# Shifting the operands of the dense layers against the weights in SBUF, and halving the products of one projection

## The reference

```
for i in range(2):                       # first block
    h = h + mixer_i(h)                   # RWKV + Hyena, then neighbourhood attention
    u = dwconv(rmsnorm(h) @ w_up)        # 1024 -> 5632, "conv_ffn"
    h = h + (gelu(u[:, :2816]) * u[:, 2816:]) @ w_down      # 2816 -> 1024
    h = h + sigmoid(rmsnorm(h) @ w_gate) * (p[i] @ w_proj)  # "ple": 1024 -> 1024, 256 -> 1024
for l in range(2):                       # second block
    x = x + gt1 * (attention(...) @ w_out)
    h = rms_norm(x) * (1 + sc2) + sh2
    x = x + gt2 * (square(relu(h @ w_mlp_in)) @ w_mlp_out)  # 1024 -> 4096 -> 1024, "mlp"
```

## Time and profile before

| | |
|---|---|
| time, median of 2 runs | 3125.95 us (3125.25 to 3126.65) |
| span of the profiled execution | 3120.8 us, on the one core |
| what the median has beyond that span | 5.15 us |
| PE busy | 2937.9 us, 94% |
| PE weight loads busy | 2328.9 us, 75% |
| DVE busy | 1717.0 us, 55% |
| ACT busy | 1294.5 us, 41% |
| HBM read | 280.57 MB, 91 GB/s over the span |

### The profile page before, as it was taken

How to read it: one execution, slowest core, us unless ns; L and a number is a source line. 1 busy time by engine, 2 the same in 40 slices (tenths; PEclk the granted TensorE clock), 3 DMA queues, 4 the chain that set the end, 5 groups by cost and what they waited for, 6 DMA issues and landing times. The chain is left out here.

```text
span 3120.8 us, 50278 instructions
## 1 busy us (share of the span) xinstructions
PE 2937.9 (94%) x21510; PEld 2328.9 (75%) x21510; DVE 1717.0 (55%) x2343; ACT 1294.5 (41%) x1998; POOL 120.0 (4%) x215
## 2 busy tenths in 40 slices
PE   7997777899999999999999899999999999999999
PEld 5764666678887777778888786678888876678887
DVE  5436665467674485657674468553333477442333
ACT  3232443243334433643233446645243446553241
POOL 0200000010000000000000010100000101000000
PEclk9998888899999999999999999999999999999999
DMA  4220000255652222245652230022233320123322
GB/s 148 81 75 13 4 4 4 82 161 191 193 153 94 88 81 95 82 132 179 219 172 91 70 108 31 1 81 95 95 95 108 90 71 1 35 89 107 95 95 81
DMA packets 223981, 287.99 MB, mean 92 GB/s; under 512 B 7967, under 2 KB 163911, under 8 KB 217616
## 3 DMA queue, kind: packets, MB, share of 16 engines
q1 hardware_dynamic: 213728, 226.26, 23.2%
q0 software_dynamic: 8448, 54.34, 5.2%
q10 hardware_dynamic: 1584, 4.19, 0.4%
HBM read 280.57 MB, written 2.10 MB: 91 GB/s over the span
## 5 line engine op out<-in xcount | busy, mean ns | idle before, releaser
L232 DVE TENSOR_TENSOR weights_low_all<-weights,weights_high_all 128x2048 fp32r<-128x2048 f32 x195 | 446.6, 2291 | 476.6 <-ACT weights_high_all L226 468.9
L226 ACT CAST weights_high_all<-weights 128x2048 fp32r<-128x2048 f32 x195 | 372.1, 1908 | 542.8 <-PE ps L240 542.8
L238 PE MATMUL ps<-ffn_h_high,weights_high_all 128*128 128x512 f32 x704 | 275.4, 391 | 0.9 <-DVE weights_low_all L232 0.9
L240 PE MATMUL ps<-ffn_h_high,weights_low_all 128*128 128x512 f32 x704 | 274.0, 389 | 0.0
L239 PE MATMUL ps<-ffn_h_low,weights_high_all 128*128 128x512 f32 x704 | 274.0, 389 | 0.0
L238 PE MATMUL ps<-mlp_h_high,weights_high_all 128*128 128x512 f32 x512 | 200.9, 392 | 0.4 <-DVE weights_low_all L232 0.3
L239 PE MATMUL ps<-mlp_h_low,weights_high_all 128*128 128x512 f32 x512 | 199.7, 390 | 0.0
L240 PE MATMUL ps<-mlp_h_high,weights_low_all 128*128 128x512 f32 x512 | 199.6, 390 | 0.0
L238 PE MATMUL ps<-weights_high_all,mlp_hid_high 128*128 128x512 f32 x512 | 199.2, 389 | 0.0
L239 PE MATMUL ps<-weights_low_all,mlp_hid_high 128*128 128x512 f32 x512 | 199.2, 389 | 0.0
L240 PE MATMUL ps<-weights_high_all,mlp_hid_low 128*128 128x512 f32 x512 | 199.2, 389 | 0.0
(11 more groups left out here) (562 smaller groups left out, 6189.4 us busy)
## 6 DMA issues: line engine op xcount, KB each, us to landing
mod_w<-in_w_mod POOLq DMA_DIRECT2D x48, 1024.0 KB, 5.3
weights<-in_ffn_w_up SPq DMA_DIRECT2D x88, 512.0 KB, 5.4
weights<-in_w_mlp_in SPq DMA_DIRECT2D x32, 1024.0 KB, 5.4
weights<-in_w_mlp_out SPq DMA_DIRECT2D x32, 1024.0 KB, 5.0
weights<-in_ffn_w_down SPq DMA_DIRECT2D x24, 768.0 KB, 4.4
weights<-in_mix_w_in SPq DMA_DIRECT2D x13, 1024.0 KB, 5.2
weights<-in_na_w_qkv SPq DMA_DIRECT2D x12, 1024.0 KB, 5.0
weights<-in_w_in SPq DMA_DIRECT2D x12, 1024.0 KB, 5.3
```

The costliest lines, as they stand in the source:

```text
L226: nc.scalar.copy(st.high[s][:], st.raw[s][:]).then_inc(st.high_done, 1)
L232: nc.vector.tensor_tensor(st.low[s][:], st.raw[s][:], st.high[s][:], ALU.subtract).then_inc(st.split_done, 1)
L238: nc.tensor.matmul(out, lh, rh, start=start, stop=False)
L240: return nc.tensor.matmul(out, ll, rh, start=False, stop=stop)
```

## The change

Buffers are put between the operands, so that `ffn_h`, `ffn_hid`, `mlp_h` and `mlp_hid` no longer lie at the same place modulo 512 as the weights. `apart` allocates an unused tile of the given number of bytes ahead of the next operand. `shifted_parts` allocates parts that are 32 bytes longer and uses them from byte 16 on. The layers get different values. In `ple_phase`, for layer 0 alone, the projection's matmuls have 256 moving columns instead of 512, twice as many of them, each with its own weight load.

```diff
-def ple_phase(nc, cx, tag, norm, split, p_in):
+def ple_phase(nc, cx, tag, norm, split, p_in, narrow):
...
-                                mm = split_product(nc, bank, src, w, start=(k == 0 and q != 1),
-                                                   stop=(k == n - 1 and q != 0))
+                                cuts = ((0, 256), (256, 512)) if q == 2 and narrow else ((0, 512),)
+                                for a, b in cuts:
+                                    mm = split_product(nc, bank[:, a:b], src, tuple(part[:, a:b] for part in w),
+                                                       start=(k == 0 and q != 1 and a == 0), stop=(k == n - 1 and q != 0 and b == 512))
...
+        def apart(scope, name, size):
+
+            scope.enter_context(nc.sbuf_tensor(f"{name}_apart", [P, size // 4], F32))
+
+        def shifted_parts(scope, name, tiles=KT):
+
+            whole = [scope.enter_context(nc.sbuf_tensor(f"{name}_{n}", [P, tiles * L + 8], F32R)) for n in ("high", "low")]
+            return [w[:, 4:tiles * L + 4].rearrange("p (k l) -> p k l", l=L) for w in whole]
...
-                h, hid = parts(hx, f"ffn_h{l}"), parts(hx, f"ffn_hid{l}", 11)
+                apart(hx, f"ffn_h{l}", (16, 64)[l])
+                h = parts(hx, f"ffn_h{l}")
+                apart(hx, f"ffn_hid{l}", (32, 16)[l])
+                hid = parts(hx, f"ffn_hid{l}", 11)
...
-                ple_phase(nc, cx, f"ple{l}", norm, h, d["p"][l, 0])
+                ple_phase(nc, cx, f"ple{l}", norm, h, d["p"][l, 0], narrow=(l == 0))
...
-                    h = parts(hx, f"mlp_h{l}")
-                    hid = parts(hx, f"mlp_hid{l}", 16)
+                    if l == 0:
+                        apart(hx, f"mlp_h{l}", 96)
+                        h = parts(hx, f"mlp_h{l}")
+                        apart(hx, f"mlp_hid{l}", 32)
+                        hid = parts(hx, f"mlp_hid{l}", 16)
+                    else:
+                        h, hid = shifted_parts(hx, f"mlp_h{l}"), shifted_parts(hx, f"mlp_hid{l}", 16)
```

## The result

The changed kernel takes 3156.21 us (median of 2 runs, 3155.06 to 3157.36) against 3125.95. The ratio on record is 1.0099 with a 95% interval of 1.0082 to 1.0115 (the two medians alone give 1.0097). The profiled execution took 3155.06 us and its span is 3153.3 us, 32.5 us more than before. The forecast was 3149.7 us, range 3100 to 3172; the change is under two per cent, the outcome that the forecast gave 0.91.

What follows compares the result with a forecast made beforehand. PE's matmul pitch alone was taken to bound the dense stages. Terms of 15.7 + 1.9 + 5.1 + 1.0 = 23.7 us took the span from 3120.8 to 3144.5 and, with 5.15 us outside it, the time to 3149.7 us; range 3100 to 3172.

Steps and rivals of the forecast that it cites:

- Point 1: ffn 0 up, ffn 1 down, mlp 0 up at offsets 32 and 96: 2352 matmuls 6.67 ns slower each, 15.7 us.
- the rival that it came from something else: The projection's 233.3 ns comes from, say, its short group's position, so offsets cost nothing; part of nothing moves, chance 0.20.
- Point 2: ffn 0 down, ffn 1 up, mlp 0 down at offsets 64 and 128: 2352 matmuls at 0.8 ns, 1.9 us.
- 64 bytes behave like 32: Sign of a wrong prediction in the dense stages: offset 64 costs as much as 32, then 10 us more.
- Point 3: mlp 1 at offsets 16, 48, 80 and 112: 1536 matmuls at 3.3 ns, the middle of 0 and 6.67, 5.1 us.
- Point 4: Projection in ple 0: 48 matmuls become 96 of 256 columns, 11.2 us becomes 12.2, +1.0 us.
- Nothing moves: Rival for the dense stages: streams fall into step at any offset, only the halved projection costs, 3127 us; chance 0.20.
- All at one step: Dense stages: every offset other than zero costs 6.67 ns, 41.6 us, 3169 us; upper end of the forecast's 0.52.
- The faster side: Rival for the dense stages: offsets keep load and matmul apart, 220 ns gives 3085 us, 215 ns 3054; chance 0.23.
- 236 ns would be the slowest stretch: Upper bound for offsets 32 and 96: +9.3 ns, 236, the slowest pitch the disturbed stretch hints at.

Runs made afterwards that it cites:

- The control: Kernel before with every part of ffn_h, ffn_hid, mlp_h and mlp_hid 512 bytes longer, still at the weights' place modulo 512; ratio 0.9994.
- the ffn kernel: Kernel before with the changed kernel's placing in the two ffn layers alone, mlp and projection as before; ratio 1.0047, interval 1.0033 to 1.0061.
- the two odd places: Kernel before with the projection's stationary parts moved to a multiple of 256 bytes from the weights and the latents' weights stepped 2048 bytes instead of 1664; ratio 1.0003.
- the second sign's kernel: Kernel before with longer parts at h / hid offsets 384 / 384, 448 / 448, 480 / 480 and 192 / 16; 3173.29 us.
- 40 stretches: Dense stretches of five kernels, the kernel before with parts 512 bytes longer, used from various bytes; ratio 0.9994 at offset zero, others 3153.07, 3173.29, 3165.79, 3151.38 us.
- The short loads: Kernels with fewer than 128 stationary columns in mlp down-projections: 64 and 32 (3126.64 us), 96 to 1 (3131.99), 64 and 32 at other distances (3129.93).

## Why the prediction was right, and where it was off

*What bounds the kernel.* Right: PE's pitch passed one to one into the span, PE had no idle time in the dense stages, and the tiles that moved under ACT and DVE cost nothing. The control and the ffn kernel show it by themselves.

*Point 1, offsets 32 and 96 at the projection's 6.67 ns.* Right, 15.7 us forecast and 15.7 measured (6.8 + 3.9 + 5.0). The one row that differed from its neighbours in nothing but an address was the right row to take, and the rival that it came from something else fell when the projection itself was moved. That 96 bytes would cost as much as 32 was a choice that came out (233.3 up, 234.3 down).

*Point 2, offsets 64 and 128.* This term was mis-sized: 1.9 us forecast, 10.0 measured (3.4 + 2.2 + 4.4), outside the bound of 0 to 1.7 ns a matmul. I took the latents as the sample for multiples of 64. They have offsets of 128 bytes from k to k, but the last edit of the two odd places shows that their pitch doesn't come from there, and a mixture of four distances would not have been a sample of one in any case. The prediction named as a sign of being wrong that 64 bytes behave like 32. In the down-projection they do (233.3 ns for both), in the up-projection of `ffn` 1 they cost a third of that (229.0). The step from the latents to offsets of 64 and 128 bytes is the one that failed, and its size, 8.1 us, stayed small against the range.

*Point 3, offsets 16 to 112 in mlp 1.* 5.1 us forecast, 5.1 measured. That is luck: the middle of two settled values was a choice and not a finding, and single stretches at offsets that are no multiple of 32 lie between 226.7 and 237.9.

*Point 4, the projection.* +1.0 forecast, +0.2 measured. The part on top was assumed to stay at 20.0 ns for each half; it was 11.6.

*The sum.* 23.7 us forecast, 31.0 measured by pitch, and point 2, 8.1 us short, is more than all of the difference. I also added 5.15 us for what lies outside the span. In the profiled execution after it is 1.8 us (3155.06 less 3153.3), and most of the 5.15 was the spread between runs of the kernel before, which goes from 3118 to 3133 us in 32 runs. The prediction also said that a measurement can tell about two per cent from no change; the interval on record, 1.0082 to 1.0115, tells one per cent from none.

*The rivals.* Nothing moves: no. All at one step, 3169 us: the second sign's kernel, 3173, is close to that, with pitches that make 37.7 us where this rival has 41.6. The faster side found no offset in 40 stretches. That 236 ns would be the slowest stretch was too low: 237.9 exists at 4 bytes.

*The mechanism.* The prediction said that load and moving operand read SBUF at the same time and that the extra is a matter of step. That the pair of addresses matters is shown, and so is that the states settle. That the load's reads take time from the moving operand's is not: the extra didn't fall with the columns loaded. The Trainium skill, TensorE: Matmul & The Clock Gate, Part 2 (Step-by-step), says that loading takes no bandwidth from the running matmul. The short loads do not speak against it (231.1 ns with one column, 226.7 with 128). The offsets do show that the two operands are not independent of each other (226.7 ns at zero, 233.3 at 32 bytes). What stays open is what the start of an fp32r matmul waits for. A stream with no load at all was not tried.

## What to carry over

Keep the stationary and the moving operand of an fp32r stream at a multiple of 256 bytes from each other (no distance tried was faster for matmuls of 512 columns), and look at every small tile (a row of sums, a gate) that is allocated ahead of one of them: it is worth 3% of a stage that PE bounds, 5% at the worst offset here. Read the pitch from starts, in every stage, and ask of two stages with the same instructions why they differ; the answer may be an address. Don't cost a term from a row that mixes several cases when a term of its own size hangs on it.

## What was not expected of the hardware

- Settled pitches are multiples of 6.67 ns or, over a few matmuls that repeat, means of them: 226.7, 228.9, 230.0, 231.1, 231.7, 233.3 ns are 34, 34 1/3, 34 1/2, 34 2/3, 34 3/4 and 35 of them. `ffn` 1 down in the changed kernel repeats every seven matmuls (237, 238, 230, 235, 235, 233, 232 ns, together 1640 ns or 246 steps, 234.3 each). In the trace of before, the starts in all stretches at 226.7 ns have the same remainder by 6.667 ns, up to a slow drift: 6.3 ns at 38 us, 4.3 at 649, 3.0 at 1507 and 0.9 at 2781. Stretches that are tens of microseconds and a pause apart thus stand on one common grid.
- The same instructions at the same addresses settled at 228.9 in one round and 233.3 in the next (`mlp` 0 up at 64 bytes), at 226.7 and 231.1 (`mlp` 0 up at 112), and at 233.3 and 228.9 before and after an interruption (`ffn` 1 up in the `ffn` kernel).
- At zero distance the extra of a matmul depends neither on its own columns (13.3 ns with 512, 13.2 with 256) nor in any simple way on the columns loaded (13.3 ns with 128, 15.6 with 112, 16.7 with 96 and 64, 18.3 with 32, 17.8 with 16 and 1).
